# Differential attention on one core: the query norm as a row factor of the masking pass, weight turns after the second panel, next head's scores ahead of the output turns

## The reference, cut to what matters

```python
q = rope(rmsnorm(two_map_heads(aq), q_norm_g), cos, sin)
k = rope(rmsnorm(two_map_heads(ak), k_norm_g), cos, sin)
lam = jnp.exp(jnp.sum(lq1 * lk1)) - jnp.exp(jnp.sum(lq2 * lk2)) + lam_init
...
sc = jnp.einsum('bhqrd,bhkrd->bhrqk', qb, k).astype(jnp.float32) * scale
p = jax.nn.softmax(jnp.where(causal, sc, -jnp.inf), axis=-1)
a = p[:, :, 0] - lam * p[:, :, 1]
return jnp.einsum('bhqk,bhkd->bhqd', a.astype(v.dtype), v)
...
oa = rmsnorm(oa, attn_norm_g) * (1.0 - lam_init)
oa = oa.transpose(0, 2, 1, 3).reshape(bsz, s, A_WIDTH) * jax.nn.silu(az)
ya = oa @ w_out_a
```

## Time and profile before

| | |
|---|---|
| median of three runs | 3376.96 us (3376.45 to 3382.3) |
| the profiled execution | 3382.91 us |
| its span, first to last instruction | 3381.1 us |
| TensorE busy | 3251.9 us, 96% of the span |
| VectorE busy | 1437.8 us, 43% |
| ScalarE busy | 820.0 us, 24% |
| GpSimd busy | 1821.1 us, 54% |
| mean granted TensorE clock | 0.986 |

### The profile page before, as it was taken

How to read it: one execution, slowest core, us unless ns; L and a number is a source line. 1 busy time by engine, 2 the same in 40 slices (tenths; PEclk the granted TensorE clock), 3 DMA queues, 4 the chain that set the end, 5 groups by cost and what they waited for, 6 DMA issues and landing times.

```text
span 3381.1 us, 47060 instructions
## 1 busy us (share of the span) xinstructions
PE 3251.9 (96%) x15456; PEld 2691.9 (80%) x15456; DVE 1437.8 (43%) x2325; ACT 820.0 (24%) x1773; POOL 1821.1 (54%) x1028
## 2 busy tenths in 40 slices
PE   5998999998998999999999999999899999999998
PEld 4877888886777888878887887888788888878887
DVE  7777462117776642126666112111166662121011
ACT  4554332014554331022222002101122220021020
POOL 3444455663444555655455665666554555656664
PEclk9999999999999999999999999999999999999999
DMA  3222222222221222232222222222222222222322
GB/s 106 75 89 67 69 75 81 98 98 63 87 87 57 76 73 89 98 102 84 75 84 78 90 96 88 94 99 95 83 84 84 75 83 87 99 87 94 99 93 99
DMA packets 87983, 290.54 MB, mean 86 GB/s; under 512 B 12833, under 2 KB 13537, under 8 KB 87921
## 3 DMA queue, kind: packets, MB, share of 16 engines
q1 hardware_dynamic: 75024, 273.12, 24.3%
q10 hardware_dynamic: 12896, 16.64, 1.8%
HBM read 275.00 MB, written 2.10 MB: 82 GB/s over the span
## 4 chain that ended last, share of the span: by engine, by line
PE 87%; DVE 7%; issue 3%; ACT 1%; ACTq 1%; DVEq 0%; DMA 0%
PE bank L556 27%; PE bank L558 27%; PE bank L557 27%; PE bank L624 1%; DVE xq L1416 1%; PE bank L742 1%; PE bank L605 1%; PE bank L653 1%; DVE k_hi L1347 1%; ACTq L1032 1%; PE bank L775 1%; DVE xk L1416 1%; DVE xn L1356 0%; DVE xk L1412 0%; PE bank L715 0%
## 5 line engine op out<-in xcount | busy, mean ns | idle before, releaser
L537 POOL TENSOR_SCALAR w_hi<-raw 128x1024 fp32r<-128x1024 f32 x512 | 560.6, 1095 | 1493.7 <-DMA raw<-in_w_in 1026.9
L540 POOL TENSOR_TENSOR w_lo<-raw,w_hi 128x1024 fp32r<-128x1024 f32 x512 | 1260.4, 2462 | 42.7
L556 PE MATMUL bank<-h_lo,w_hi 128*128 128x512 f32 x2816 | 1118.4, 397 | 0.6 <-DVE h_lo L1359 0.3
L558 PE MATMUL bank<-h_hi,w_hi 128*128 128x512 f32 x2816 | 1099.9, 391 | 0.0
L557 PE MATMUL bank<-h_hi,w_lo 128*128 128x512 f32 x2816 | 1098.7, 390 | 0.0
L558 PEld LDWEIGHTS bank<-h_hi,w_hi 128*128 128x128 f32 x2816 | 530.4, 188 | 113.2
L556 PEld LDWEIGHTS bank<-h_lo,w_hi 128*128 128x128 f32 x2816 | 531.4, 189 | 108.8 <-issue 2.5
L557 PEld LDWEIGHTS bank<-h_hi,w_lo 128*128 128x128 f32 x2816 | 531.6, 189 | 106.0
L1373 DVE TENSOR_TENSOR x<-x,bank 128x512 f32 x64 | 44.0, 688 | 458.1 <-PE bank L558 458.1
L556 PE MATMUL bank<-w_lo,up_hi 128*128 128x512 f32 x512 | 199.2, 389 | 0.0
L557 PE MATMUL bank<-w_hi,up_lo 128*128 128x512 f32 x512 | 199.2, 389 | 0.0
(11 more groups left out here) (297 smaller groups left out, 4520.1 us busy)
## 6 DMA issues: line engine op xcount, KB each, us to landing
raw<-in_w_in SPq DMA_DIRECT2D x288, 512.0 KB, 3.3
raw<-in_w_up SPq DMA_DIRECT2D x64, 512.0 KB, 3.3
raw<-in_w_down SPq DMA_DIRECT2D x64, 512.0 KB, 3.2
raw<-in_w_out_a SPq DMA_DIRECT2D x16, 512.0 KB, 3.2
raw<-in_w_out_b SPq DMA_DIRECT2D x16, 512.0 KB, 3.3
raw<-in_w_o SPq DMA_DIRECT2D x16, 512.0 KB, 3.2
raw<-in_p_ret SPq DMA_DIRECT2D x16, 512.0 KB, 3.3
raw<-in_p_sb SPq DMA_DIRECT2D x16, 512.0 KB, 3.3
```

Of the source, the lines that this page charges most:

```text
L537: nc.gpsimd.tensor_scalar(m.w_hi[:, slot], m.raw[:, slot], 1.0, 0.0, ALU.mult, ALU.add).then_inc(s["w_step"], 1)
L540: nc.gpsimd.tensor_tensor(m.w_lo[:, slot], m.raw[:, slot], m.w_hi[:, slot].bitcast(F32), ALU.subtract).then_inc(s["split"], 1)
L556: nc.tensor.matmul(dst, hi, rhs_lo, start=first, stop=False, **more)
L558: return nc.tensor.matmul(dst, hi, rhs_hi, start=False, stop=last, **more)
```

## The change

- Query norm: `rotate_qk(0, ...)` no longer multiplies by the inverse norm. `group_sum(0, ...)` takes, for each of the four blocks of 128 tokens, the squares as the stationary operand and two columns of the ones-and-zeros matrix as the moving one, for low and high part: eight matmuls that leave eight columns with tokens on the partitions. `group_rstd(0, ...)` works on these eight columns with three small activations, the last of which multiplies by minus the softmax scale. `maxima` takes its scale from such a column in place of a constant. VectorE's `weights` waits for `rstd_ready`.
- `combine` is one function for all four blocks: it waits for all exponentials, takes one reciprocal of eight columns and one small product of four, then runs the four wide instructions in the order of blocks 3, 2, 1, 0. The order of `maxima` and of the exponentials becomes 2, 0, 3, 1.
- All `weight_turns` move behind the second panel and behind `group_sum(0, 1)`; all `values` move behind `group_sum(1, 1)`. ScalarE's three `turned_out` move behind `group_rstd(0)`.
- The scores of the next head are issued in the current turn, between the fourth panel and `output_turns`; those of the first head ahead of the loop. The pairs of score blocks are reordered, and only the last pair waits for `on_ready`.
- VectorE's `rotate_qk(0, 1)` moves ahead of `split_squares(1, 1)`.

```diff
--- before.py
+++ after.py
@@ -175,13 +175,13 @@

 PE_MISC_L1 = 50
 PE_MISC_L2 = 20
-ACT_L1 = 133
-ACT_A = 8
+ACT_L1 = 141
+ACT_A = 9
 ACT_B = 10
 ACT_L2 = 96
 ACT_R = 7
-DVE_L1 = 335
-DVE_A = 22
+DVE_L1 = 279
+DVE_A = 15
 DVE_B = 28
 DVE_L2 = 196
 DVE_R = 33
@@ -435,9 +435,9 @@
                m.bank[2 + k][:, 0:512]] for k in range(2)]

         groups = ((3,), (2,), (0, 1))
-        order = (3, 1, 2, 0)
+        order = (2, 0, 3, 1)
         turn = [m.bank[2][:, 0:512], m.bank[4][:, 0:384], m.bank[6][:, 0:384]]
-        pairs = ((1, 3), (3, 2), (2, 1), (0, 0))
+        pairs = ((3, 1), (2, 2), (0, 0), (1, 3))
         pv = m.bank[3]
         xb = [m.bank[2 + i] for i in range(TB)]
         block = ctx.enter_context(nc.Block())
@@ -630,20 +630,28 @@
                 lo, hi = ((m.sql_q, m.sqh_q), (m.sql_k, m.sqh_k))[which]
                 pe.wait_ge(s["sq_split"], at.at("a", ahead, times=2) + (which + 1))
                 misc_bank()
-                nc.tensor.matmul(misc[:], m.grp[:], lo[:], start=True, stop=False)
-                nc.tensor.matmul(misc[:], m.grp[:], hi[:], start=False, stop=True).then_inc(s["ss_done"], 1)
+                if which == 1:
+                    nc.tensor.matmul(misc[:], m.grp[:], lo[:], start=True, stop=False)
+                    mm = nc.tensor.matmul(misc[:], m.grp[:], hi[:], start=False, stop=True)
+                else:
+                    for b in range(TB):
+                        tok = slice(b * P, b * P + P)
+                        nc.tensor.matmul(misc[:, 2 * b:2 * b + 2], lo[:, tok], m.grp[:, 0:P:64], start=True, stop=False)
+                        mm = nc.tensor.matmul(misc[:, 2 * b:2 * b + 2], hi[:, tok], m.grp[:, 0:P:64], start=False,
+                                              stop=True)
+                mm.then_inc(s["ss_done"], 1)

             def value_turns(ahead):
                 pe.wait_ge(s["vT_ready"], at.at("a", ahead + 1))
                 misc_bank()
                 turn4(misc, lambda b: m.vT[:, b * P:b * P + P]).then_inc(s["vT_done"], 1)

-            def scores():
-                pe.wait_ge(s["qk_ready"], at.at("a", 1, times=2))
-                pe.wait_ge(s["on_ready"], at.at("a", 1))
+            def scores(ahead):
+                pe.wait_ge(s["qk_ready"], at.at("a", ahead + 1, times=2))
                 for both in pairs:
-                    if both[1] == 1:
-                        pe.wait_ge(s["score1_done"], at.at("a", 1))
+                    if both[1] == 3:
+                        pe.wait_ge(s["score1_done"], at.at("a", ahead + 1))
+                        pe.wait_ge(s["on_ready"], at.at("a", ahead + 1))
                     for part in range(3):
                         for k, qb in enumerate(both):
                             r = slice(64 * k, 64 * k + 64)
@@ -651,14 +659,14 @@
                             q = m.q_lo if part == 1 else m.q_hi
                             key = m.k_lo if part == 0 else m.k_hi
                             mm = nc.tensor.matmul(sq[k][qb], q[r, tok], key[r, keys], start=part == 0, stop=part == 2)
-                            if part == 2 and both == pairs[0] and k == 0:
+                            if part == 2 and (k, qb) == (1, 1):
                                 mm.then_inc(s["score1_done"], 1)
-                            elif part == 2 and both in pairs[1:] and (k, qb) in ((0, 3), (1, 1), (1, 0)):
+                            elif part == 2 and (k, qb) in ((1, 0), (1, 3)):
                                 mm.then_inc(s["scores_done"], 1)

             def weight_turns(g):

-                pe.wait_ge(s["a_ready"], at.at("a", times=TB) + (1, 3, 4)[g])
+                pe.wait_ge(s["a_ready"], at.at("a", times=TB) + (1, 2, 4)[g])
                 start = QOFF[groups[g][0]]
                 for qb in groups[g]:
                     for sb in range(qb + 1):
@@ -850,24 +858,22 @@
                 group_sum(1, 0)
                 value_turns(0)
                 gate_rows()
+                scores(0)
                 with at.loop(A_HEADS - 1, panel=4, acc=4, a=1, misc=4):
-                    scores()
-                    h_gemm()
-                    weight_turns(0)
+                    h_gemm()
                     h_gemm()
                     group_sum(0, 1)
-                    weight_turns(1)
-                    values(0)
-                    weight_turns(2)
+                    for g in range(len(groups)):
+                        weight_turns(g)
                     h_gemm()
                     group_sum(1, 1)
-                    values(1)
-                    values(2)
+                    for g in range(len(groups)):
+                        values(g)
                     value_turns(1)
                     h_gemm()
+                    scores(1)
                     output_turns()
                     at.add("a")
-                scores()
                 h_gemm()
                 for g in range(len(groups)):
                     weight_turns(g)
@@ -1040,9 +1046,16 @@

             def group_rstd(which, sq_buf, ahead):
                 act.wait_ge(s["ss_done"], at.at("a", ahead, times=2) + (which + 1))
-                own(activation(sq_buf[:], misc[:], ACT.Ln, bias=m.col[:, 2:3], scale=1.0 / A_DH))
-                act.sem_inc(s["misc_free"], 1)
-                activation(sq_buf[:], sq_buf[:], ACT.Exp, scale=-0.5).then_inc(s["rstd_ready"], 1)
+                if which == 1:
+                    own(activation(sq_buf[:], misc[:], ACT.Ln, bias=m.col[:, 2:3], scale=1.0 / A_DH))
+                    act.sem_inc(s["misc_free"], 1)
+                    activation(sq_buf[:], sq_buf[:], ACT.Exp, scale=-0.5).then_inc(s["rstd_ready"], 1)
+                else:
+                    rows = m.sm[:, 84:92]
+                    own(activation(rows, misc[:, 0:2 * TB], ACT.Ln, bias=m.col[:, 2:3], scale=1.0 / A_DH))
+                    act.sem_inc(s["misc_free"], 1)
+                    own(activation(rows, rows, ACT.Exp, scale=-0.5))
+                    activation(rows, rows, ACT.Copy, scale=-(A_DH ** -0.5)).then_inc(s["rstd_ready"], 1)

             def values_out(ahead):
                 act.wait_ge(s["vT_done"], at.at("a", ahead + 1))
@@ -1055,7 +1068,7 @@
                     act.wait_ge(s["max_ready"], at.at("a", times=TB) + (j + 1))
                     w = slice(QOFF[qb], QOFF[qb] + (qb + 1) * P)
                     for k, p in enumerate((m.p0, m.p1)):
-                        i = 2 * j + k
+                        i = 2 * qb + k
                         ins = activation(p[:, w], p[:, w], ACT.Exp, bias=m.sm[:, 20 + i:21 + i], scale=-1.0,
                                          accum_out=m.sm[:, 28 + i:29 + i])
                     ins.then_inc(s["p_ready"], 1)
@@ -1207,13 +1220,12 @@
                     log_exp_tables()
                     exponentials()
                     qk_out(0, m.xq, m.sq_q)
-                    turned_out(0)
                     rotate_halves(m.rot_q, m.xq, s["rot_q_in"], 32)
                     qk_out(1, m.xk, m.sq_k)
                     rotate_halves(m.rot_k, m.xk, s["rot_k_in"], 32)
                     group_rstd(0, m.sq_q, 1)
-                    turned_out(1)
-                    turned_out(2)
+                    for g in range(len(groups)):
+                        turned_out(g)
                     copy_out(m.vT, s["vT_ready"])
                     group_rstd(1, m.sq_k, 1)
                     values_out(1)
@@ -1425,42 +1437,44 @@
                 x, rot, sqb = ((m.xq, m.rot_q, m.sq_q), (m.xk, m.rot_k, m.sq_k))[which]
                 dve.wait_ge(s["rot_k_in" if which else "rot_q_in"], at.at("a", ahead + 1, times=64))
                 rotate(x, rot, m.cos, m.sin,
-                       (sqb, (s["rstd_ready"], at.at("a", ahead, times=2) + (which + 1))))
+                       (sqb, (s["rstd_ready"], at.at("a", ahead, times=2) + 2)) if which else None)
                 hi, lo = ((m.q_hi, m.q_lo), (m.k_hi, m.k_lo))[which]
                 split(hi[:], lo[:], x[:], s["qk_ready"])

             def maxima(i):

                 qb = order[i]
-                if i < 3:
-                    dve.wait_ge(s["scores_done"], at.at("a", times=3) + (i + 1))
+                if i % 2 == 0:
+                    dve.wait_ge(s["scores_done"], at.at("a", times=2) + (i // 2 + 1))
                     dve.sem_inc(s["rows_begun"], 1)
                 for k, p in enumerate((m.p0, m.p1)):
                     ins = nc.vector.tensor_tensor_reduce(
                         p[:, QOFF[qb]:QOFF[qb] + (qb + 1) * P], sq[k][qb], m.mq_row[:, (TB - 1 - qb) * P:],
-                        op0=ALU.add, op1=ALU.min, scale=-(A_DH ** -0.5), scalar=-BIG_NEG,
-                        accum_out=m.sm[:, 20 + 2 * i + k:21 + 2 * i + k])
+                        op0=ALU.add, op1=ALU.min, scale=m.sm[:, 84 + 2 * qb + k:85 + 2 * qb + k], scalar=-BIG_NEG,
+                        accum_out=m.sm[:, 20 + 2 * qb + k:21 + 2 * qb + k])
                 ins.then_inc(s["max_ready"], 1)

-            def combine(i):
-
```

(29 more changed lines are left out.)

## The result

| | before | after |
|---|---|---|
| median | 3379.1 us (4 runs) | 3465.7 us (4 runs, 3463.2 to 3470.3) |
| ratio | | 1.0258, 95% interval 1.0242 to 1.0274 |
| span of the profiled execution | 3381.1 us | 3468.5 us |
| mean granted TensorE clock | 0.986 | 0.975 |

The change makes the kernel 2.6% slower. The prediction said slower, with the wait that does it, but 1.4%, and its range ended at 3450.

What follows compares the result with a forecast made beforehand. TensorE, busy for 96% of the span, bounds the kernel. Twelve heads +37, first heads -2, tails +3, clock +10: +48, rounded down to +46 on 3382.9, giving 3423 us, 1.4% above the median 3377.0; range 3395 to 3450.

Steps and rivals of the forecast that it cites:

- T + 11.8: TensorE's second panel ends and wants group_sum(0) 11.8 us after T, the start of the output turns; before, T + 14.2.
- T + 10.0 and T + 15.6: GpSimd starts splitting the next panel at T + 10.0; the one after is requested at T + 15.6.
- rival 1: VectorE passes GpSimd's split without being held: wait at group_sum(0) only 0.9 us, about 3375 us, no change; chance 0.08.
- rival 2: Scores cover the o_sb wait and the query squares are in time: -1.3 us a head, 3355 us; chance 0.10.
- rival 3: Wide products not held but the square split is: wait 2.9 us, +1.8 a head, 3400 us; shares slower's 0.82.
- The forecast's own case: GpSimd holds VectorE's wide combine products; squares ready at T + 16.0, TensorE waits 4.2 us at group_sum(0); chance 0.70.
- `maxima` starts at T + 3.6: First step of VectorE's chain after T, taken from the last head, where it meets GpSimd in head_branch.
- the bad case: GpSimd's next panel slips in ahead of the square split's last instruction: upper bound 5.3 us for the group_sum(0) wait.
- starts from free engines: First head of each layer: saves small waits and o_sb, about -2 a layer less 0.9 for group sums, together -2.
- for the tails I put +3 us: Tails: gate_rows behind combine, T + 11.5 for T + 10.4; erow wait grows 1.2 to 1.5 us a layer.
- The clock: Half-clock stretches after TensorE's waits in ten of twelve heads: +17 less the present 7, +10 us; bounds -7 and +14.
- The keys' wait of 0.2 us: At group_sum(1): keys ready at T + 23.3, wanted at T + 23.4; 0.2 us a head, 0 to 1.2.

Runs made afterwards that it cites:

- experiment 1: The changed kernel with the next head's scores put back behind the output turns, all else as changed: 3393.8 us, ratio 1.0033 against the kernel before.
- experiment 8: The kernel before with the scores ahead of the output turns alone, score pairs ordered as in the change: 3429.3 us, ratio 1.0156.
- experiment 10: The changed kernel with VectorE's maxima of the next head ahead of head_branch: 3390.5 us, ratio 1.0014 against the kernel before.
- experiment 5: The changed kernel with GpSimd's L540 cut to 8 of 1024 columns, TensorE's amount of work unchanged: 3379.3 us, ratio 0.9999 against the kernel before.
- experiment 4: The changed kernel with 16 additional useless matmuls ahead of the sql_q wait in each of 14 heads: 3450.3 us, ratio 1.0191 against the kernel before.
- experiment 2: The changed kernel with combine taken apart again block by block, each waiting only for its own exponentials: 3497.5 us, ratio 1.0343 against the kernel before.

## Why the prediction was right in direction and wrong in size

**The mechanism was right in outline.** The waits for `o_sb` went, a wait at the first matmul of `group_sum(0)` came, and experiments 1, 8 and 10 tie it to the scores ahead of the turns with VectorE's chain behind them. The second panel was forecast to end at T + 11.8 and ended at T + 11.4; GpSimd was forecast at T + 10.0 and T + 15.6 and came there; the exponentials took 229.4 - 224.9 = 4.5 us. Rivals 1 (engines that miss each other) and 2 (faster) fell: the engines met in all twelve heads, and TensorE waited at `group_sum(0)` in each.

**Which instruction is held was wrong in eleven heads of twelve.** The prediction named as a sign of being wrong that the four wide products keep their 0.75, 0.6, 0.5 and 0.35 us, and they did: 1.94 us together. What L540 held was the small product ahead of them, which the sum had at its free 0.2 us, and the third panel held the last instruction of the split in nine heads. So rival 3 was right that the wide products are free and the split is held, though by the third panel and not by L540; its wait of 2.9 us came out too short, as it too started `maxima` at T + 3.6. The forecast's own case, the wide products held to the end of L540, came with its 4.2 us in the head at 182.36 alone, the only one in which `maxima` started in time.

**The wait was mis-sized, 4.2 against 5.5 us** in the twelve heads ((74.0 - 7.9) / 12). The step that failed is the first of the chain, "`maxima` starts at T + 3.6". I took it from a head in which GpSimd's panel caught one instruction of `head_branch` for a short time. With the scores ahead, GpSimd's L537 starts 0.15 us before `a_hi` (0.01 to 0.32 in the eleven heads), so that L537 holds `a_hi` and L540 holds `a_lo` to its end: T + 5.6, and 5.4 to 5.7 in the others. Experiments 5 and 10 confirm it from two sides. I had even named the meeting, and priced it by the milder row. In that row L537 comes 3.8 us behind the fourth panel, at T + 2.1. With turns 2.1 us behind the panel in place of 1.7 it comes at T + 1.7, on `a_hi` itself. And the trace before holds the harder case, which I overlooked, in the head at 834.55, where L537 came at T + 1.7 ahead of `a_hi` and `maxima` started at T + 5.8. The slack of that head hid it:

```profile
837.73 2.66 DVE L1348 TENSOR_TENSOR a_lo<-sz,a_hi 128x512 f32 x1
840.31 0.68 DVE L1439 CUSTOM_DVE_ANT_0 p<-bank,mq_row 128x512 f32<-128x512 f32 x1
```

The two later holds partly made up for it: VectorE came so late that only the end of the second panel's split caught it. The third panel, which stood in the bounds as the bad case, did hold the last instruction. So the wait in the head shown was 5.85, and in nine heads of twelve it was beyond my upper bound of 5.3.

**Two terms were missed.** I gave the first head of each layer no such wait ("starts from free engines"). It waits 3.9 us: ScalarE's `gate_rows` stands ahead of its exponentials, so they start only at 71.95 and combine meets the first split (its four wide products take 4.81 us). This was not new: in the trace before, in the first layer, they started at 69.92, the split of the query squares took 1.28 and 2.76 us, and TensorE waited 0.7 us for it. The engines were not free. And for the tails I put +3 us for the longer chain, with combine done at T + 11.5, as if GpSimd held nothing there. It was held as in the heads and ended at T + 15.4. The first weight turns stand behind one panel alone, with no scores ahead of it, and wait 8.2 us: tails cost (16.4 + 6.4) - 14.5 = 8.3 us less the former 1.3 for p.

**The clock was mis-sized, +10 against about +35 us.** I reckoned one stretch of 3.4 us for a wait, taken from waits of 1.7 us, and that in ten of twelve heads. It came in all 14, and in 13 of them it was 6.5 us or longer. In the head shown it was 10.2 us, and TensorE was busy for 7.6 of them, so one wait cost up to 3.7 us by the clock, 2.9 in the mean, and not 1.7. Experiment 4 shows the direction and the lower part of the size, 15 to 23 us, with the filler not covering the whole wait. This is the largest single error of the sum.

**The sum redone.** Forecast +48; the waits of the twelve heads 66.1 in place of 50.4, +16; the first heads +8; the tails +4; the clock +25; the keys' wait that did not show, -2; the rest of the program -9. That is +90, where the two profiled executions differ by 87.

**Smaller terms.** The eight narrow matmuls took 0.9 us at full clock (192.86 to 193.77 in the run of experiment 4), as estimated, and 1.7 at 1.2 GHz. The keys' wait of 0.2 us did not show; it was hidden. It was real, though: with the wait for the queries gone it was 1.5 us in 12 heads (experiments 1 and 10). The rule of the Trainium skill, "GPSIMD Engine Reference", section 1, that instructions with two SBUF inputs contend with GpSimd, is agreed to by the trace: GpSimd held a product of four columns for 2.00 us as it held one of 512 for 2.66. My sum had left that small product out.

## What to carry to other kernels

When work is moved ahead of a hand-over, reckon the slack of every other chain that starts at it: here 2 us less between turns and second panel turned 3.0 us of slack, seen in no list of waits, into a wait of 5 in each head, together with the holds that the new places brought. Where a second engine can hold an instruction, price it by its worst alignment, and put into the stretch in which it runs those instructions that it cannot hold, here `maxima`, which read PSUM and took the same 0.75 us beside GpSimd. A wait of several us also costs the clock behind it, which in this kernel came to more than half of the waiting that was added.

## What the runs showed of the hardware that I had not expected

- A held instruction is not held for less because it is small: 128x4 took 2.00 us in place of 0.22, and in experiment 2 one of 128x1 took 0.81 behind L537 and up to 2.12 behind L540. Which engine starts first decides who is held, down to the last digit of the trace: with L537 and `a_hi` both at T + 1.70 (the head at 182.36) `a_hi` took 0.43, and with L537 0.01 us ahead (the head at 970.79) it took 1.31.
- After a wait of 5.85 us the granted clock stayed at 0.51 for 10.2 us, although TensorE was busy for 7.6 of them, one of the three longest of 14 such stretches, where the usual one is 6.5 to 7 us; 224 matmuls of no use made the kernel 15 us faster.
- Shortening one GpSimd instruction of each panel in the kernel before, with TensorE's work unchanged, gave 1.5%, more than all TensorE's waits for `o_sb` (0.6%). TensorE's waits over the whole program fell by 44 us in the two traces, the span by 58.
